# One block for the first projections, and attention joined with its output projection

## The chip, the cores and the metric

The kernel runs on one core of one Trainium2 chip. The metric is the device time of one execution in microseconds (us). The engines are named as in the profile: PE is the matrix engine (PEld its weight loads), DVE the vector engine, ACT the scalar engine, POOL the GpSimd engine, SP the engine that here only issues DMAs. Each engine works through its own instruction queue in order; between engines there are semaphores.

## The reference

One encoder layer over 1280 tokens (1024 of a prompt, 256 of a sample), width 1024, in float32:

```python
h = rmsnorm(x, g_mix)
q, k, v, z, xbc, dtf, dtb, ga, gs = split(h @ w_in)
ya = windowed_gqa(q, k, v, sink, bias) @ w_attn_out     # 8 heads, 2 KV heads, window +-128
ys = ssd_branch(z, xbc, dtf, dtb, conv...) @ w_ssd_out  # conv over time, bidirectional scan, gated norm
x = x + (sigmoid(ga) * ya + sigmoid(gs) * ys) @ w_out
x = x + hier_moe(rmsnorm(x, g_ffn))                     # 16 experts, 2 per token
x = x + sigmoid(rmsnorm(x, g_ple) @ w_ple_gate) * (p @ w_ple_proj)
return rmsnorm(x, g_final)
```

The change lies in the first two lines of the mixers: the projections of `h`, the attention, and the product with `w_attn_out`.

## The kernel before

Every float32 product is made of three passes: each operand is split into a high part (a rounded copy) and a low part (the rest), and high x high, high x low and low x high are summed in PSUM. Weights come in units of 128 x 1024 numbers (512 KB). For each unit SP loads the raw numbers, ACT copies the high part (`split`), and POOL subtracts to get the low part (`rest`, a TENSOR_TENSOR). A ring of two slots (`raw`, `whi`, `wlo`, built by `weight_ring`) carries the units; a slot is loaded again when POOL has read it.

The stages run in this order, each inside a block of its own. At the end of a block every engine waits until all have finished, and a stage usually has its SP queue wait for its last stores before that.

1. `stage_norm_project_z`: normalises and transposes `h`, then multiplies it with eight resident units of `z` in 24 tiles (three groups of token tiles times eight channel tiles), `silu` on ACT after each, and stores them. After tile 19 PE makes the 32 `dt` channels, and after the last tile it transposes them; DVE copies the result to `dt_raw` (L1169).
2. `stage_project_conv`: ten channel tiles of `xbc` (`product`, 8 k-tiles x 3 passes x 3 column groups of 512, 512 and 256 tokens), a convolution on DVE, `silu` on ACT, transposes on PE. Then two "early" tiles of the next stage's columns. It starts with a warm-up of PE (L176) while the first units are loaded and split.
3. `stage_project_rest`: twenty more tiles of the same kind (`q`, `k`, `v` and the gates), two PSUM buffers. Woven into PE's order are small products for the scan's decays: `product(0)`, `decays.tensor`, `product(1)`, `decays.tensor_rows`, and so on. `decays.tensor` waits for a chain of about sixteen small DVE and ACT steps (`Decays.vector`, L555 to L574), which itself waits for two small parameter loads, `dec_bias` and `dec_alog` (L540, L541). POOL's order is `rest(2)`, `rest(3)`, `pool_line`, `rest(4)`, ... where `pool_line` (L766, L770) waits for a line of the bias table that PE makes after `product(3)`.
4. `stage_attention`: PE warms up, makes the scores of unit 0 (a unit is a token tile and half of the heads; there are 20), transposes V in ten steps with two PSUM banks, and makes the scores of unit 1. DVE makes the statistics of unit 0 (`stats`), then copies the ten V tiles (L1404), then makes the statistics of unit 1. ACT takes the exponentials of a unit when its statistics are ready. In the loop, PE transposes the probabilities, ACT copies them out, PE weighs V with them, DVE scales. The attention result of a token tile is turned by PE (`out`), its high part taken by ACT and its low part by DVE. POOL splits the first two units of `w_attn_out` here (`next_hi`, `next_lo`); SP loads them at token tile 1.
5. All semaphores are cleared between two barriers (`clear_semaphores`, L134).
6. One block for `stage_out_att`, the scan and what follows. `stage_out_att` has eight channel tiles of 4 k-tiles x 3 passes over all 1280 tokens; SP loads a gate row, ACT takes its sigmoid (after loading the Sigmoid table, L1458), DVE multiplies (L1494, L1496). PE's tile c waits for DVE's tile c-2.

Several stage functions can add code to one block: then each engine runs the first function's instructions and goes on to the second's with no barrier between.

## Time and profile before

| | us |
|---|---|
| median of 3 runs | 1876.85 (1872.38 to 1877.21) |
| the profiled execution | 1874.15 |
| its span | 1872.3 |
| PE busy in the span | 1743.8 (93%) |
| DVE, ACT, POOL busy | 893.0, 596.7, 410.5 |

Times in the rows below are counted from the start of the span; 1.85 us of the profiled execution lie outside it. The columns PEclk in a table of stretches and in the page give the TensorE clock that was granted: 1.00 is 2.4 GHz and 0.50 is 1.2 GHz. A bracket at the end of a row says how long the engine sat idle before it and what ended the wait.

### The profile page before, as it was taken

To read this page: it belongs to the slowest core of one execution; us is meant where nothing else is said; L and a number is where in the kernel's file an instruction comes from. 1 tells how busy PE (TensorE), PEld (TensorE's weight loads), DVE (VectorE), ACT (ScalarE), POOL (GpSimd) and SP (SyncE) were. 2 spreads that over 40 slices of the span, in tenths; PEclk is the share of its full clock that TensorE was granted. 3 is DMA by queue.
4 is the path that set the end of the run, shared out by engine and by line. 5 is a ranking of instruction groups with operands and counts; after the bars stand their busy time and mean duration, and the time that the engine had idled before them with its cause. 6 is when DMAs were issued, how large, how long until landed. Compare 5 with 4: busy or idle time off the path is not lost. (4 is left out here: it accounts for less than half of the span.)

```text
span 1872.3 us, 27121 instructions
## 1 busy us (share of the span) xinstructions
PE 1743.8 (93%) x10458; PEld 1430.1 (76%) x10459; DVE 893.0 (48%) x1037; ACT 596.7 (32%) x1001; POOL 410.5 (22%) x278
## 2 busy tenths in 40 slices
PE   6998999898999979989999999998899998998897
PEld 5876888786877757768788888787677876786686
DVE  5200777301133216751488522512767787940675
ACT  4201222231111115652355412312534443443332
POOL 3001111112111110001010013000155555652330
PEclk8999999999999989989899999999899998998899
DMA  5212222223345421006666344323857776752552
GB/s 195 88 34 69 68 84 76 106 62 123 117 156 175 130 91 40 28 10 191 201 190 192 115 139 147 101 74 90 314 192 269 255 284 235 296 191 97 173 191 90
DMA packets 115836, 265.90 MB, mean 142 GB/s; under 512 B 13011, under 2 KB 59555, under 8 KB 115740
## 3 DMA queue, kind: packets, MB, share of 16 engines
q1 hardware_dynamic: 99484, 209.11, 34.1%
q0 software_dynamic: 8320, 30.43, 4.8%
q10 hardware_dynamic: 7936, 25.01, 3.7%
q8 instruction: 70, 1.15, 0.3%
q14 instruction: 26, 0.21, 0.0%
HBM read 192.95 MB, written 71.55 MB: 141 GB/s over the span
## 5 line engine op out<-in xcount | busy, mean ns | idle before, releaser
L2078 DVE TENSOR_TENSOR ex_wlo<-ex_raw,ex_whi 128x1024 fp32r<-128x1024 f32 x102 | 168.6, 1667 | 6.0 <-ACT ex_whi L2072 6.0
L286 PE MATMUL rest_p<-hi_h,whi_in 128*128 128x512 f32 (+1 forms) x480 | 123.3, 366 | 12.1 <-POOL wlo_in L905 6.7
L2655 PE MATMUL rt_p<-ex_whi,ex_xh 128*128 x280 | 115.6, 413 | 13.8 <-issue 7.5
L2074 DVE CAST ex_whi<-ex_raw 128x1024 fp32r<-128x1024 f32 x96 | 95.4, 999 | 65.2 <-DMA ex_raw<-experts 60.6
L286 PE MATMUL rest_p<-lo_h,whi_in 128*128 128x512 f32 (+1 forms) x480 | 120.9, 361 | 0.0
L286 PE MATMUL rest_p<-hi_h,wlo_in 128*128 128x512 f32 (+1 forms) x480 | 120.7, 360 | 0.0
L2657 PE MATMUL rt_p<-ex_whi,ex_xl 128*128 x280 | 111.7, 399 | 0.0
L2656 PE MATMUL rt_p<-ex_wlo,ex_xh 128*128 x280 | 111.6, 398 | 0.0
L286 PEld LDWEIGHTS rest_p<-hi_h,whi_in 128*128 128x128 f32 x480 | 81.1, 191 | 34.4 <-POOL wlo_in L905 7.6
L876 ACT ACTIVATE rest_out<-rest_p 128x1024 f32<-128x1024 f32 x20 | 20.5, 1025 | 256.6 <-PE rest_p L286 256.6
L905 POOL TENSOR_TENSOR wlo_in<-wraw_in,whi_in 128x1024 fp32r<-128x1024 f32 x18 | 43.7, 2431 | 222.0 <-ACT whi_in L870 222.0
L286 PEld LDWEIGHTS rest_p<-lo_h,whi_in 128*128 128x128 f32 x480 | 80.7, 190 | 14.4
L286 PEld LDWEIGHTS rest_p<-hi_h,wlo_in 128*128 128x128 f32 x480 | 80.5, 190 | 14.3
L2611 POOL TENSOR_TENSOR ex_xl<-ex_xs,ex_xh 128x1024 fp32r<-128x1024 f32 x35 | 85.9, 2455 | 14.5 <-ACT ex_xs L2057 13.9
L468 DVE SCALAR_TENSOR_TENSOR conv_acc<-xpad,conv_w,conv_acc 128x1284 f32<-128x1284 f32 x40 | 81.7, 2042 | 5.0 <-DVE conv_acc L464 0.3
L1285 PEld LDWEIGHTS pv_p<-v_tok,probs_t 128*128 128x128 f32 x480 | 62.1, 198 | 25.1 <-ACT probs_t L1338 15.2
L1285 PE MATMUL pv_p<-v_tok,probs_t 128*128 128x65 f32 x480 | 68.4, 281 | 10.8 <-ACT probs_t L1338 7.9
L2655 PEld LDWEIGHTS rt_p<-ex_whi,ex_xh 128*128 128x128 f32 x280 | 53.9, 193 | 31.9 <-issue 21.3
L286 PE MATMUL xbc_p<-hi_h,whi_in 128*128 128x512 f32 (+1 forms) x288 | 72.7, 361 | 2.2 <-POOL wlo_in L412 2.2
L1117 PE MATMUL z_p<-hi_h,z_hi 128*128 128x512 f32 (+1 forms) x192 | 70.6, 368 | 4.4 <-DVE lo_h L1151 4.4
L286 PE MATMUL xbc_p<-lo_h,whi_in 128*128 128x512 f32 (+1 forms) x288 | 71.9, 358 | 0.0
L286 PE MATMUL xbc_p<-hi_h,wlo_in 128*128 128x512 f32 (+1 forms) x288 | 71.8, 358 | 0.0
(387 smaller groups left out, 4049.7 us busy)
## 6 DMA issues: line engine op xcount, KB each, us to landing
ex_raw<-experts SPq DMA_DIRECT2D x96, 512.0 KB, 6.2
wraw_in<-units SPq DMA_DIRECT2D x36, 512.0 KB, 4.0
y_slots<-ex_y ACTq DMA_DIRECT2D x35, 512.0 KB, 3.7
rest<-rest_out SPq DMA_DIRECT2D x20, 640.0 KB, 5.7
scan_e<-erow SPq DMA_DIRECT2D x32, 256.0 KB, 4.5
xtok<-conv_tok SPq DMA_DIRECT2D x10, 640.0 KB, 3.3
z_x<-x SPq DMA_DIRECT2D x10, 512.0 KB, 4.1
ao_gate<-rest SPq DMA_DIRECT2D x8, 640.0 KB, 5.2
```

Source lines behind the costliest of these rows:

```text
L286: mm = pe.matmul(out[:, n, 0:size], w[:, kk, :], h[:, kk, c:c + size], start=(kk == 0 and w is whi and h is hi), stop=(kk == ktiles - 1 an ...
L468: mm = dve.scalar_tensor_tensor(out=cv[:, s, :], in0=xpad[:, s, w:w + CONV_LEN], scalar=cw[:, ds(c, 1), w:w + 1], in1=cv[:, s, :], op0=ALU ...
L876: act.activation(got[:, s, 0:1024].rearrange("p (a n) -> p a n", a=2), gp[s][:, 0:2, :], ACT.Copy)
L905: pool.tensor_tensor(wlo[:, s, :], raw[:, s, :], whi[:, s, :].bitcast(F32), ALU.subtract).then_inc(w_lo, 1)
L1117: pe.matmul(out, w.hi[u][:, col], hi[:, kk, tok], start=(kk == 0), stop=False)
L1285: mm = pe.matmul(pv[:, i, :], pt[:, j % 4, b * P:(b + 1) * P], vn[:, n + n // QB + b, i // 2, :], start=(b == 0), stop=(b == 2))
L2074: eng.tensor_copy(self.hi[:, e % 2, n, :], self.raw[e % 2][:, n, :]).then_inc(self.w_hi[n], 1)
L2078: eng.tensor_tensor(self.lo[:, e % 2, n, :], self.raw[e % 2][:, n, :], self.hi[:, e % 2, n, :].bitcast(F32), ALU.subtract).then_inc(self.w ...
L2611: pool.tensor_tensor(xl[s][:, :, :], xs[s][:, :, :], xh[s][:, :, :].bitcast(F32), ALU.subtract).then_inc(x_lo, 1)
L2655: pe.matmul(gu[s][:, :], xh[s][:, kk, :], hi, start=(kk == 0), stop=False)
L2656: pe.matmul(gu[s][:, :], xh[s][:, kk, :], lo, start=False, stop=False)
L2657: mm = pe.matmul(gu[s][:, :], xl[s][:, kk, :], hi, start=False, stop=(kk == KT - 1))
```

## The change

The stages `z`, `conv` and `rest` become one block. The semaphores are cleared after it, and attention moves into the block of `stage_out_att`. Between the stages there are now semaphores where the barriers were:

- the first two `xbc` units are loaded and split within the `z` stage after tile 19, and their low parts made on POOL; the warm-up before `xbc` is gone;
- the first product of `rest` waits for what the `conv` stage left in its PSUM buffers and ring; its two loads follow on SP's queue, each after POOL has read the slot (`first_lo`);
- POOL's `rest(4)` stands ahead of `pool_line`;
- V is copied by ACT; SP loads the first `w_attn_out` units at token tile 3;
- tiles 0 and 1 of `stage_out_att` are made by column groups: columns 0 to 1023 before the last token tile of attention is turned (`last_out`), columns 1024 to 1279 after.

```diff
 stage_project_conv
+        def load_first(sp):
+            for n in range(2):
+                sp.dma_start(raw[:, n, :], d["units"][U_XBC + n]).then_inc(w_in[n], 16)
+        def split_first(act):
+            for n in range(2):
+                act.wait_ge(w_in[n], 16)
+                act.activation(whi[:, n, :], raw[:, n, :], ACT.Copy).then_inc(w_hi, 1)
+        z_tile, z_silued, z_stored, dt_kept = project_z(load_first, split_first)
...
-            sp.wait_ge(stored[0], 96)
-            sp.wait_ge(stored[1], 96)
-            sp.wait_ge(early_stored, 16 * EARLY)
...
-            act.preload_act_table(ACT.Silu)
...
+            rest(0, 0)
+            rest(1, 1)
+            pool.wait_ge(z_tile, 24)
             pool.memset(xpad[:, :, :], 0.0).then_inc(pads, 1)
...
-            warm_up(pe, k, gp[0][:, 0, :], 4)
             product(0, 0, first=True)
+            pe.wait_ge(z_silued, 24)
+            pe.wait_ge(dt_kept, 1)
 stage_project_rest
-            load(2, 0)
-            load(3, 1)
+            for s in range(2):
+                sp.wait_ge(first_lo, 2 + 12 + s + 1)
+                load(2 + s, s)
             decays.sync(sp)
...
             decays.scalar_first(act)
+            act.wait_ge(early_stored, 16 * EARLY)
             copy(0, 0, 1)
...
             rest(2, 0)
             rest(3, 1)
+            rest(4, 0)
             tables.pool_line(pool)
-            with pool.Fori(2, n_tiles // 2) as i:
+            rest(5, 1)
+            with pool.Fori(3, n_tiles // 2) as i:
...
-                pe.wait_ge(w_lo, c + 3)
-                pe.wait_ge(copied, c + 1)
+                if c < 2:
+                    pe.wait_ge(first_lo, 2 + 12 + c + 1)
+                    pe.wait_ge(early_copied, c + 1)
+                else:
+                    pe.wait_ge(w_lo, c + 3)
+                    pe.wait_ge(copied, c + 1)
...
             product(0, 0)
+            pe.wait_ge(tok_copied, 33)
             decays.tensor(pe)
 stage_norm_project_z
+                if n == 19:                        # SP
+                    sp.wait_ge(tile_done, 20)
+                    load_next(sp)
...
+                if n == 20:                        # ACT
+                    act.wait_ge(tile_done, 20)
+                    split_next(act)
                 silu(n)
 stage_attention
-            sp.wait_ge(v_zero, 2)
+            sp.wait_ge(v_zero, 1)
...
-                if n == 1:
+                if n == 3:
                     for u in range(2):
                         sp.dma_start(next_raw[:, u, :], d["units"][U_AO + u]).then_inc(next_in, 16)
...
-            out(NT - 1)
+        def last_out(pe):
+            n = NT - 1
+            pe.wait_ge(att_done, 2 * n + 2)
+            pe.wait_ge(att_lo_s, n)
+            for m in range(4):
+                mm = pe.transpose(ap_[:, m, :], att[:, n % 2, m * P:(m + 1) * P], ident)
+            mm.then_inc(att_turned, 1)
...
+            act.wait_ge(ones_set, 1)               # ACT, ahead of its unit loop
+            for t in range(NT):
+                act.wait_ge(v_turned, t + 1)
+                at = t + 1 if t < QB else t + 2
+                act.activation(vn[:, at, :, 0:HEAD], tp[t % 2][:, 0:P].rearrange(...), ACT.Copy).then_inc(v_copied, 1)
...
             stats(0)
-            for t in range(NT):                    # DVE
-                ...
-                dve.tensor_copy(vn[:, at, :, 0:HEAD], tp[t % 2][:, 0:P].rearrange(...)).then_inc(v_copied, 1)
             stats(1)
 stage_out_att
+        sp.wait_ge(att_turned, 4 * 2 * NT)
         load_gate(0)
...
+        def part(c, n):
+            size = 512 if n < 2 else 256
+            ...
+            for kk in range(4):
+                for a, b in ((w, hi), (w, lo), (wl, hi)):
+                    mm = pe.matmul(gp[c][:, n, 0:size], a[:, kk, :], b[:, kk, 512 * n:512 * n + size], ...)
+        pe.wait_ge(first_split, 4)
+        pe.wait_ge(att_lo_s, 8)
+        for c in range(2):
+            for n in range(2):
+                part(c, n)
+        last_out(pe)
+        pe.wait_ge(att_lo_s, NT)
+        for c in range(2):
+            part(c, 2).then_inc(mm_done, 1)
+        for c in range(2, KT):
-        for c in range(KT):
 build
-    stage_norm_project_z(k, hi, lo)
-    stage_project_conv(k, hi, lo, ring)
-    stage_project_rest(k, hi, lo, q, ring)
+    with k.nc.Block() as block:
+        ...                                        # z, conv and rest, all in this block
-    stage_attention(k, att_hi, att_lo, ring)
     k.clear_semaphores()
...
+                    done = stage_attention(k, inner, block, att_hi, att_lo, ring)   # inside the block after
```

## Rows read from the trace of the kernel before

**Rows 1.** Timeline (start, duration, engine, operation, idle before): from `z` to `conv`.
```profile
124.53 0.60 ACT L1054 ACTIVATE z_out<-z_p 128x512 f32<-128x512 f32 x1 [4.84 <-PE z_p L1119]
160.93 0.49 DVE L1169 COPY dt_raw<-dt_p 128x320 f32<-128x320 f32 x1 [61.37 <-PE dt_p L1135]
171.36 0.85 PE L286 MATMUL xbc_p<-hi_h,whi_in 128*128 128x512 f32 x3 [2.21 <-POOL wlo_in L412]
```

**Rows 2.** Timeline: from `conv` to the first products of `rest`.
```profile
353.91 2.34 POOL L412 TENSOR_TENSOR wlo_in<-wraw_in,whi_in 128x1024 fp32r<-128x1024 f32 x1 [12.78 <-ACT whi_in L366]
356.90 1.41 PE L286 MATMUL rest_p<-hi_h,whi_in 128*128 128x512 f32 x3 [5.34 <-ACTq L863]
358.12 0.43 SPq L541 DMA_DIRECT2D dec_alog<-a_log  x1
362.41 0.49 DVE L555 TENSOR_TENSOR dec_w<-dt_raw,dec_bias 128x320 f32<-128x320 f32 x1 [5.72 <-DMA dec_alog<-a_log]
371.72 0.33 DVE L574 TENSOR_SCALAR ssd_dta<-ssd_minus_dta 128x320 f32<-128x320 f32 x1
373.16 1.25 PE L627 MATMUL rest_spare<-ssd_dta,const 128*128 128x160 f32 x6
374.00 0.98 PE L286 MATMUL rest_p<-hi_h,whi_in 128*128 128x512 f32 x3
...
388.39 0.28 PE L645 MATMUL rest_spare<-const,ssd_dta 128*16 128x128 f32 x1
```

**Rows 3.** Busy time by engine, granted clock, DMA share, GB/s in one stretch.
```profile
356.00:360.00 4.00, 3.10 (x8) 2.58 (x9) 0.07 (x1) 1.28 (x1) 0.24 (x1) 0.50 0.51 146
```

**Rows 4.** Timeline: the stall of tile 4 of `rest`.
```profile
407.56 1.06 ACT L870 ACTIVATE whi_in<-wraw_in 128x1024 fp32r<-128x1024 f32 x1
...
429.28 1.44 PE L286 MATMUL rest_p<-hi_h,whi_in 128*128 128x512 f32 x3 [6.72 <-POOL wlo_in L905]
```

**Rows 5.** Line views of both barriers of the clearing (count, duration, first and last start).
```profile
L136 SPq DRAIN  x3: 7/7/7, 841.5 to 1724.0; - x3
L138 SPq EVENT_SEMAPHORE  x3: 17/17/17, 843.0 to 1725.1; - x3
```

**Rows 6.** Waits of PE, whole span: us, times, longest.
```profile
PE att_tp L1305 <- DVE v_tok L1404: 6.5, 4, 6.0
```

**Rows 7.** Timeline: attention's first units.
```profile
693.36 0.44 PE L1305 MATMUL att_tp<-const,v_ch 128*128 128x128 f32 x2
699.54 2.13 ACT L1330 ACTIVATE scores<-scores,att_stat 128x384 f32<-128x384 f32 x4 [13.53 <-DVE att_stat L1377]
702.97 2.93 PE L1264 MATMUL score_p<-k_win,q_blk 64*128 64x384 f32 x8
705.95 1.76 DVE L1367 SCALAR_TENSOR_TENSOR scores<-score_p,bias 128x1536 f32<-128x1536 f32 x1 [2.58 <-PE score_p L1264]
```

**Rows 8.** Line views (count: shortest, median, longest ns) in attention.
```profile
L1338 ACT ACTIVATE probs_t<-att_tp x80: 465/490/493, 706.6 to 833.0; 128x384 f32<-128x384 f32 x80
L1377 DVE TENSOR_TENSOR att_stat<-att_stat,sink x20: 161/161/2189, 697.3 to 826.2; 128x4 f32<-128x4 f32 x20
```

**Rows 9.** Timeline: POOL's subtraction beside that line.
```profile
697.12 2.37 POOL L1251 TENSOR_TENSOR wlo_in<-wraw_in,whi_in 128x1024 fp32r<-128x1024 f32 x1
```

**Rows 10.** Timeline: end of attention and the first output tiles.
```profile
835.18 1.06 PE L1295 MATMUL att_t<-const,att_tok 128*128 128x128 f32 x4
839.54 0.60 ACT L1342 ACTIVATE hi_att<-att_t 128x512 fp32r<-128x512 f32 x1 [2.67 <-PE att_t L1295]
...
843.06 1.28 ACT L1458 ACT_TABLE_LOAD   x1 [2.92 <-PEq L138]
849.77 1.27 ACT L1461 ACTIVATE ao_gate<-ao_gate 128x1280 f32<-128x1280 f32 x1 [0.27 <-DMA ao_gate<-rest]
858.99 1.23 DVE L1494 TENSOR_TENSOR ao_prod<-ao_p,ao_gate 128x1024 f32<-128x1024 f32 x1 [5.48 <-PE ao_p L286]
860.13 0.41 DVE L1496 TENSOR_TENSOR ao_prod<-ao_p,ao_gate 128x256 f32<-128x256 f32 x1
```

More of the change, by code:

```diff
@@ L288, in pe_channel_tile, with stage_project_conv @@
     return mm
-def stage_project_conv(k, hi, lo, ring):
+def stage_project_conv(k, ctx, block, hi, lo, ring, project_z):
     nc, d = k.nc, k.d
-    with ExitStack() as ctx:
+    if True:
         raw, whi, wlo = ring
@@ L458, in _ @@
             dve.wait_ge(cw_in, 16)
+            for s in range(4):
+                dve.wait_ge(z_stored[s], 96)
             def conv(c, s):
@@ L487, in _ @@
             tokens(9, 1, 4)
+    return stored, ch_stored, early_copied, early_stored, w_lo, tok_copied
 class SsdTiles:
@@ L802, in vector, with stage_project_rest @@
         dve.memset(bias[:, 2, :, 2 * P:], NEG)
-def stage_project_rest(k, hi, lo, q, ring):
+def stage_project_rest(k, ctx, block, hi, lo, q, ring, xt_stored, ch_stored, early_copied, early_stored, first_lo, tok_copied):
     nc, d = k.nc, k.d
     n_tiles = 22 - EARLY
-    with ExitStack() as ctx:
+    if True:
         raw, whi, wlo = ring
         got = k.at("rest_out", [P, 2, T], F32, O_ST)
+        gp = [ctx.enter_context(nc.psum_tensor(f"rest_p{s}", [P, 3, 512], F32)) for s in range(2)]
         spare = [ctx.enter_context(nc.psum_tensor(f"rest_spare{n}", [P, 512], F32)) for n in range(2)]
@@ L917, in _ @@
             decays.vector(dve)
+            dve.wait_ge(ch_stored, 16)
+            for s in range(2):
+                dve.wait_ge(xt_stored[s], 96)
             tables.vector(dve, states.free)
@@ L969, in pe_token_tile, with stage_norm_project_z @@
     return mm
-def stage_norm_project_z(k, hi, lo):
+def stage_norm_project_z(k, ctx, block, hi, lo, load_next, split_next):
     nc, d = k.nc, k.d
@@ L1168, in _, with stage_attention @@
             dve.wait_ge(dt_turned, 1)
-            dve.tensor_copy(k.dt_raw[:, :, :], dp[:, :, :])
-def stage_attention(k, att_hi, att_lo, ring):
+            dve.tensor_copy(k.dt_raw[:, :, :], dp[:, :, :]).then_inc(dt_kept, 1)
+    return tile_done, silued, stored, dt_kept
+def stage_attention(k, ctx, block, att_hi, att_lo, ring):
     nc, d = k.nc, k.d
     UNITS = 2 * NT
-    with ExitStack() as ctx:
+    if True:
         o = O_R1 + 10 * 4096
@@ L1415, in _, with stage_out_att @@
             rest(NT - 1)
-def stage_out_att(k, ctx, block, hi, lo, ring, early):
+    return last_out, att_lo_s, turned, next_split
+def stage_out_att(k, ctx, block, hi, lo, ring, early, last_out, att_lo_s, att_turned, first_split):
     nc, d = k.nc, k.d
@@ L1474, in _ @@
     def _(pe):
-        for c in range(KT):
+        def part(c, n):
+            size = 512 if n < 2 else 256
+            w, wl = (x[:, 0, c * 4 * P:(c + 1) * 4 * P].rearrange("p (k c) -> p k c", k=4) for x in (whi, wlo))
+            for kk in range(4):
+                for a, b in ((w, hi), (w, lo), (wl, hi)):
+                    mm = pe.matmul(gp[c][:, n, 0:size], a[:, kk, :], b[:, kk, 512 * n:512 * n + size],
+                                   start=(kk == 0 and a is w and b is hi), stop=(kk == 3 and a is wl))
+            return mm
+        pe.wait_ge(first_split, 4)
[8 more added lines that the diff above has]
+        for c in range(2, KT):
             u = c // 2
@@ L2991, in out_att @@
                 with ExitStack() as inner:
-                    return stage_out_att(k, inner, block, att_hi, att_lo, ring, early)
+                    done = stage_attention(k, inner, block, att_hi, att_lo, ring)
+                with ExitStack() as inner:
+                    return stage_out_att(k, inner, block, att_hi, att_lo, ring, early, *done)
             done = stage_ssd_scan(k, ctx, block, y_hi, y_lo, so_ring, out_att)
```

52 lines of the change are left out of this document (26 added, 26 removed).

## The prediction

> **What bounds the kernel now.** I read the page first: PE is busy in 93% of the span, every other engine in under half, so the kernel is paid for in PE's order of work, and what can be won cheaply is what PE idles. The waits of PE over the whole span come next; there the reader is to see that the long waits of the first half lie on few places, such as the transposes of V, which waited 6.5 us for DVE's copies [rows 6]. The timelines around those places then show who was late. Between the places PE is dense: in `conv`, in `rest` and in the output tiles a product follows a product, and work that is moved off other engines there is worth nothing. The table of stretches adds a second price: after 5.34 us of idling the first products ran at a granted clock of 0.50 [rows 2, 3], so a pause costs its own length and then a slow start. A product of `rest` at full clock takes 388.39 - 374.00 = 14.39 us, the one behind the pause 373.16 - 356.90 = 16.26: the slow start costs 1.87 [rows 2].
>
> **The change part by part.** All times are on the clock of the old trace; a gain is how much earlier PE reaches the same instruction.
>
> *From z to conv.* PE started the first `xbc` product at 171.36, after a block end, a load, a split and a subtraction on POOL [rows 1]. Now the two loads leave after tile 19, whose `silu` ran at 124.53; loading, splitting and subtracting have over 30 us beside dense PE work and cost nothing. SP's queue gets two loads, ACT two copies ahead of a `silu` that waits for PE anyhow. What is late next: the product waits for `padded`, which DVE raises only behind its copy to `dt_raw`, 160.93 + 0.49 = 161.42. With a handover of 0.2 PE starts at 161.6: gain 9.7 (10.4 with no handover and no copy in the way, 9.2 with a handover of 0.7). The clearing of `xpad` on POOL waits for the last tile, but its reader comes a product later.
>
> *From conv to rest.* The first product of `rest` started at 356.90, 5.34 after `conv` ended at 351.56 [rows 2]. Its unit was split and its buffer copied long before, so now it starts at 351.6 with a warm clock and ends at 351.6 + 14.39 = 366.0, 7.2 before the old 373.16. But `decays.tensor` is next in PE's queue and needs DVE's chain, and the chain needs `dec_alog`. On SP that load stands behind `load(3)`, which now waits for POOL's subtraction to end at 353.91 + 2.34 = 356.25; two more issues of 0.43 put it at 357.2, only 0.9 before the old 358.12. With the old flight of 362.41 - 358.12 = 4.29 it lands at 361.5; one 512 KB load fewer is right ahead, so I take 360.5. The chain lasts 371.72 + 0.33 - 362.41 = 9.64, so PE goes on at 370.2, after a pause of 4.2. `decays.tensor` took 374.00 - 373.16 = 0.84; at half clock I put 1.3, so product 1 starts at 371.5 instead of 374.00. Of these 2.5 the slow start takes 1.9 back: gain 0.5 (-0.5 with the old flight, 3.3 if the load is quick and the clock holds). So here one pause is traded for another. The added wait for `tok_copied` is long satisfied; the wait for the early stores stands in ACT's queue ahead of `copy(0)`, behind the chain's last exponential step, with the stores landed by then.
>
> *The order on POOL.* Tile 4 of `rest` waited 6.72 us because POOL sat in `pool_line`, though the high part was there at 407.56 + 1.06 = 408.6 [rows 4]. With `rest(4)` ahead, its low part is ready some 11 us before PE wants it: gain 6.72 and the slow start, 8.6 (8.0 to 8.8). `pool_line` is not delayed, since it waits for tile 3's end; `rest(5)` follows it with a whole product to spare.
>
> *The clearing.* It moves from behind attention to behind `rest`. From the first barrier to the end of the second took 843.0 - 841.5 = 1.5 us here and 1.1 at the last place [rows 5]. The old end of `rest` had a plain block end, so attention starts 1.5 later: -1.5 (-1.1 to -1.6). The clearing behind attention is counted below.
>
> *V on ACT.* ACT idled 13.53 us before the first exponentials [rows 7], so the copies are beside nothing that ends last. PE transposes V from 693.36. A copy of 128 x 128 is not in the trace; a copy three times as wide takes 0.49 [rows 8], so ten take at most 4.9 and at least a third of it, and I put 4.5 with the handovers. Then the scores of unit 1 run from 698.0, for 2.93 at half clock as before or half of that at full, and `stats(1)` starts at 699.5 to 701 instead of 705.95; the first exponentials need only `stats(0)`, and follow at 698. Gain 4.9 to 6.4; I take 5.7, and 4.5 as the lowest. `stats(1)` leads the later units, so it carries through.
>
> *The weight split inside the loop.* POOL's copies and subtractions for `w_attn_out` now fall into the unit loop. In the trace DVE's small addition L1377 took 2189 ns once against a median of 161, from 697.32 on, while POOL's subtraction ran from 697.12 to 699.49 [rows 8, 9]. ACT's exponentials waited for it [rows 7], so this is on the path. Two subtractions of 2.37 fall into a loop in which such small operations come once in (826.2 - 697.3) / 19 = 6.8 us: a chance of about 0.7, with half of 2.37 each time, is 0.8; I take -1.0 (0 to -2.4, as both can hardly be hit fully). The Trainium skill (SBUF, State Buffer, section Who interferes with whom) says that a vector operation with two SBUF inputs and a GpSimd operation that reads SBUF lock each other out whole, and one with a single SBUF input does not; by it only L1374 and L1377 are exposed and the term stays at 1.0, while without it the 1.76 us of L1367 [rows 7] could be hit too and the term would be near its end of -2.4. The row of L1377 agrees; no row here shows a safe operation beside that subtraction in the unit loop.
>
> *Attention into its projection.* The old PE finished `out(8)` at 835.18 + 1.06 = 836.24 and reached output tile 2 at 858.99, DVE's start on tile 1 [rows 10]. Now four parts of 12 passes of 512 columns follow at once: 14.39 us for 24 x 1280 columns gives 0.240 per 512 or 11.5, and 1.9 for a slow start: 849.6. Then `last_out` (0.6 at full clock) and ACT's high part (0.60) until 850.8. ACT's queue has the Sigmoid table (1.28) and the first sigmoid (1.27) only behind that: 853.4. DVE's product (1.23 + 0.41) ends at 855.0, and PE, done with its two short parts by 854.4, waits for it. Gain 4.0 (3.0 if ACT's handovers add up, 5.9 if neither the table nor the slow start shows).
>
> The sum is 9.7 + 0.5 + 8.6 - 1.5 + 5.7 - 1.0 + 4.0 = 26.0 us. From the profiled execution, 1874.15, that leaves 1848.1. This execution lies 2.7 under the median of the runs shown, from which it would be 1850.9; I predict 1849.
>
> **The rivals.**
> - *The decays are not late.* The parameter loads land early enough or the clock survives the pause: 2.8 more, 1846. For it: they are 16 KB each. Against: the queue order, which holds them to 357.2.
> - *The clock stays low through the token parts.* Attention's last transposes and weighings ran at half clock, and if the parts don't raise it, their 11.5 take 23: 9.6 more, 1859. Against: behind the pause of rows 3 dense products had it back within a product.
> - *The first stage change does nothing.* If the two units are still not split when `z` ends, 9.7 are lost: 1859. For it: the loads wait in SP's queue behind stores. Against: they have 30 us.
> - *The unbroken run is throttled.* `z`, `conv` and the start of `rest` now run without a pause: from tile 19 at 124.53 to 366 that is over 240 us, where `conv` alone ran 351.56 - 171.36 = 180 [rows 1, 2]. If the granted clock fell to half beyond 180, the last 60 would take 120: 60 - 26 = 34 slower, 1908. It decides from a mean grant under 60 / (60 + 26) = 0.70 in those 60. For it: no row shows such a run. Against: each fall behind which I saw a slow start came after idling, as in rows 2 and 3.
>
> **How the numbers follow.** Chances: the forecast 0.68; decays in time 0.12; clock low in the parts 0.08; first change void 0.05; throttled run or a like loss 0.03; half of the gains lost in some way not named 0.04, which leaves about 1862. The low ends of the terms add to 9.2 - 0.5 + 8.0 - 1.6 + 4.5 - 2.4 + 3.0 = 20.2, the high ends to 10.4 + 3.3 + 8.8 - 1.1 + 6.4 - 0 + 5.9 = 33.7; they will not all fall on one side. From 1874.15 and from the median that spans 1840 to 1857. I give 1840 to 1859, which takes in the two rivals at 1859 and leaves out the slow one and the last. What a measurement of this kernel can tell from no change is about 0.3%, 5.6 us: faster by more 0.95, within 0.02, slower 0.03.
>
> **What would show it.** Right: no warm-up and under 1 us of PE idling between the `dt` transposes and `xbc`; PE waiting some 4 us for DVE at `decays.tensor` with the grant at 0.50 behind it; no wait of tile 4 for POOL; V's transposes running through within 5 us; DVE's L1374 or L1377 once near 1 to 2 us; PE dense from `out(8)` to output tile 2 but for about 2 us. Wrong: a pause elsewhere of the same size as one removed, above all inside `rest` or at the start of the scan, or a granted clock under 1.00 in a dense stretch.

## The result, and the profile after

The changed kernel took 1843.26 us (median of 4 runs, 1834.84 to 1844.89) against 1874.62 us for the kernel before (4 runs, 1866.73 to 1877.21) on the same chip: a ratio of 0.9844, 95% interval 0.9809 to 0.9879, or some 31 us less. The forecast was 1849, 26.0 less than before. The profiled execution spans 1840.8 us where the old one spanned 1872.3.

To see where the time came from, I took the same instruction in both traces and noted how much earlier it starts now (the lead). The gain of a part is the growth of the lead across it.

| PE or ACT reaches | before | after | lead | gain of the part | predicted |
|---|---|---|---|---|---|
| first `xbc` product | 171.36 | 160.91 | 10.45 | 10.3 (`z` itself ended 0.2 earlier) | 9.7 |
| first `rest` product | 356.90 - 5.34 idle | 340.93 | 10.6 | 0.2, `conv` | 0 |
| end of tile 3 of `rest` | 421.53 | 410.44 | 11.1 | 0.5 | 0.5 |
| end of `rest`, last copy | 679.09 | 659.41 | 19.7 | 8.6 | 8.6 |
| attention's warm-up | 683.85 | 665.54 | 18.3 | -1.4 | -1.5 |
| `stats(1)` | 705.95 | 680.02 | 25.9 | 7.6 | 5.7 |
| last exponential of the unit loop | 827.95 | 803.55 | 24.4 | -1.5, of it -0.9 by the held operation | -1.0 |
| output tile 2 | 858.71 | 824.97 | 33.7 | 9.3 | 4.0 |
| end of the span | 1872.3 | 1840.8 | 31.5 | -2.2 | 0 |

Most groups of rows of the old kernel have an answer in the new trace. *From z to conv* [rows 1], timeline (start, duration, engine, line, operation, idle before and its releaser):

```profile
160.73 0.49 DVE L1200 COPY dt_raw<-dt_p 128x320 f32<-128x320 f32 x1 [61.36 <-PE dt_p L1166]
160.91 0.83 PE L286 MATMUL xbc_p<-hi_h,whi_in 128*128 128x512 f32 x3 [0.22 <-DVEq L463]
```

No warm-up and no wait for POOL is left: PE idles 0.22 us, for the increment that stands in DVE's queue behind the `dt_raw` copy.

*From conv to rest* [rows 2], the same view:

```profile
340.93 0.75 PE L286 MATMUL rest_p<-hi_h,whi_in 128*128 128x512 f32 x3
...
346.74 0.42 SPq L554 DMA_DIRECT2D dec_alog<-a_log  x1
350.42 0.49 DVE L568 TENSOR_TENSOR dec_w<-dt_raw,dec_bias 128x320 f32<-128x320 f32 x1 [22.53 <-DMA dec_alog<-a_log]
359.73 0.33 DVE L587 TENSOR_SCALAR ssd_dta<-ssd_minus_dta 128x320 f32<-128x320 f32 x1
360.20 2.47 PE L640 MATMUL rest_spare<-ssd_dta,const 128*128 128x160 f32 x6 [5.04 <-DVE ssd_dta L587]
362.00 1.74 PE L286 MATMUL rest_p<-hi_h,whi_in 128*128 128x512 f32 x3
```

And by stretches (us, busy time of PE, PE's loads, DVE, ACT, POOL, then the granted clock, DMA share, GB/s), as in [rows 3]:

```profile
340.00:355.00 15.00, 15.00 (x78) 12.62 (x76) 3.76 (x8) 4.70 (x7) 2.41 (x1) 1.00 0.39 120
...
360.00:364.00 4.00, 3.80 (x11) 3.15 (x12) 0.55 (x2) 2.56 (x5) 2.12 (x1) 0.51 0.00 0
364.00:375.00 11.00, 11.00 (x58) 9.36 (x57) 2.00 (x18) 0.00 (x0) 0.23 (x1) 1.00 0.38 109
```

The first product of `rest` runs at once at a grant of 1.00. Then PE waits 5.04 us for DVE's chain, and the grant behind the wait is 0.51, as behind the old pause. The old pause went and came back a product later.

*Tile 4 of rest* [rows 4] follows the line's product (410.44 to 411.4) without a wait:

```profile
411.39 0.85 PE L286 MATMUL rest_p<-hi_h,whi_in 128*128 128x512 f32 x3
```

*Attention's first units* [rows 7] (V's copies, the scores of unit 1, its statistics), and the place in the loop where POOL's work met DVE's [rows 9]:

```profile
675.55 0.45 ACT L1388 ACTIVATE v_tok<-att_tp 128x128 f32<-128x128 f32 x2 [7.85 <-PE att_tp L1338]
...
678.41 1.56 PE L1297 MATMUL score_p<-k_win,q_blk 64*128 64x384 f32 x8
...
679.29 2.13 ACT L1370 ACTIVATE scores<-scores,att_stat 128x384 f32<-128x384 f32 x4 [0.50 <-DVE att_stat L1423]
...
680.02 1.76 DVE L1413 SCALAR_TENSOR_TENSOR scores<-score_p,bias 128x1536 f32<-128x1536 f32 x1 [0.76 <-PE score_p L1297]
...
701.57 2.36 POOL L1283 TENSOR_TENSOR wlo_in<-wraw_in,whi_in 128x1024 fp32r<-128x1024 f32 x1
...
703.86 1.04 POOL L1281 CAST whi_in<-wraw_in 128x1024 fp32r<-128x1024 f32 x1
703.88 1.05 DVE L1420 SCALAR_TENSOR_TENSOR att_stat<-att_stat,nsink 128x4 f32<-128x4 f32 x1
```

Two of V's tiles take ACT 0.70 from start to start (675.55 to 676.25 and so on), so all ten are done in 3.2. The scores of unit 1 run in 1.56, at full clock, where the old ones took 2.93. In the loop the small operation L1420 takes 1.05 instead of 0.16, and it ends when POOL's cast does (704.90). That is a hold as forecast, but by the cast: the prediction had counted only the subtractions.

*The end of attention* [rows 10]. First the stretches from the last exponential: of the kernel after, of the kernel before, and of a second profile of the kernel before (`before_again` below):

```profile
803.60:808.50 4.90, 3.97 (x37) 3.73 (x35) 0.00 (x0) 2.37 (x7) 0.00 (x0) 1.00 0.17 32
808.50:819.50 11.00, 11.00 (x51) 9.05 (x50) 1.36 (x4) 0.60 (x1) 0.00 (x0) 1.00 0.27 107
819.50:825.00 5.50, 3.77 (x30) 3.31 (x28) 2.33 (x4) 4.32 (x4) 0.00 (x0) 1.00 0.00 0
```

```profile
827.90:839.10 11.20, 8.12 (x41) 7.49 (x38) 1.43 (x5) 3.06 (x8) 0.00 (x0) 0.56 0.00 0
```

```profile
826.60:834.30 7.70, 4.61 (x39) 4.08 (x38) 1.40 (x5) 3.04 (x8) 0.00 (x0) 1.00 0.00 0
```

The low grant of 0.56 at the old end of attention is absent from the second profile of the same kernel (1.00). So the change need not have won that part: from the last exponential to the end of `out(8)` the two old profiles take 8.3 and 5.2 us, and the new one 5.2. From the end of `out(8)` to output tile 2 they take 22.5 and 22.6, and the new one 16.2. The new handover itself, in the timeline (`last_out`'s transposes run from 819.51 to 820.1):

```profile
820.14 0.60 ACT L1382 ACTIVATE hi_att<-att_t 128x512 fp32r<-128x512 f32 x1 [10.77 <-PE att_t L1357]
820.76 1.28 ACT L1501 ACT_TABLE_LOAD   x1
...
821.52 0.38 PE L1523 MATMUL ao_p<-hi_att,whi_in 128*128 128x256 f32 x1 [1.41 <-DVE lo_att L1442]
...
823.36 1.22 DVE L1555 TENSOR_TENSOR ao_prod<-ao_p,ao_gate 128x1024 f32<-128x1024 f32 x1 [1.90 <-ACT ao_gate L1504]
...
824.97 0.85 PE L286 MATMUL ao_p<-hi_att,whi_in 128*128 128x512 f32 x3 [0.32 <-DVE ao_prod L1557]
```

*What was given back.* From the first gather of the experts to the last product of its stage the lead fell from 36.4 to 31.7. (From output tile 2 to that gather it had grown by 2.7; the second pair of profiles below does not show that growth.) The waits of PE (total, times, longest) name the place: POOL's product `ex_hid`, 8.9 us at the longest where the old kernel has 5.3. First after, then before:

```profile
PE pp_p L2741 <- POOL ex_hid L2676: 10.8, 2, 8.9
```

```profile
PE pp_p L2680 <- POOL ex_hid L2615: 7.2, 2, 5.3
```

One such product takes 11.31 us on POOL where the other 34 of this trace take 0.73 to 1.72, beside a run of casts and subtractions on DVE, which the timeline shows without a hole up to 1532.2:

```profile
1521.51 11.31 POOL L2676 TENSOR_TENSOR ex_hid<-ex_up,ex_silu 128x256 f32<-128x256 f32 x1 [7.14 <-ACT ex_up L2771]
...
1529.89 2.34 DVE L2139 TENSOR_TENSOR ex_wlo<-ex_raw,ex_whi 128x1024 fp32r<-128x1024 f32 x2
...
1542.25 0.69 DVE L2135 CAST ex_whi<-ex_raw 128x1024 fp32r<-128x1024 f32 x1 [10.01 <-DMA ex_raw<-experts]
```

In the old trace the same product took 7.17 us:

```profile
1557.17 7.17 POOL L2615 TENSOR_TENSOR ex_hid<-ex_up,ex_silu 128x256 f32<-128x256 f32 x1 [7.26 <-ACT ex_up L2710]
```

It ended inside DVE's run, beside a cast that came a little late: that cast (1563.79) began 0.03 us behind the end of the subtraction before it, while the others of that run start some 0.1 before the subtraction ends. In the second old profile the late cast still starts 0.04 before that end, and the product took 7.17 there too; so a late start goes with the way in, and a full hole is not shown to be needed.

### The profile page after: what moved, and what is told of

Read it like the earlier page. It is cut to its first block and busy times, and to the rows that moved or that the text cites. A ratio compares the mean times of both kernels' runs of the same rounds, so it can differ in the third digit from the quotient of the medians.

```text
span 1840.8 us, 27069 instructions
## 1 busy us (share of the span) xinstructions
PE 1726.6 (94%) x10450; PEld 1417.9 (77%) x10451; DVE 885.6 (48%) x1027; ACT 597.5 (32%) x1010; POOL 414.3 (23%) x278
## 3 DMA queue, kind: packets, MB, share of 16 engines
q8 instruction: 70, 1.15, 0.3%
## 5 line engine op out<-in xcount | busy, mean ns | idle before, releaser
L920 POOL TENSOR_TENSOR wlo_in<-wraw_in,whi_in 128x1024 fp32r<-128x1024 f32 x18 | 43.8, 2434 | 230.5 <-ACT whi_in L883 230.5
L2672 POOL TENSOR_TENSOR ex_xl<-ex_xs,ex_xh 128x1024 fp32r<-128x1024 f32 x35 | 85.9, 2456 | 16.2 <-ACT ex_xs L2118 15.7
L412 POOL TENSOR_TENSOR wlo_in<-wraw_in,whi_in 128x1024 fp32r<-128x1024 f32 x14 | 36.1, 2585 | 204.2 <-ACT whi_in L370 152.2
L1318 PEld LDWEIGHTS pv_p<-v_tok,probs_t 128*128 128x128 f32 x480 | 59.7, 191 | 26.6 <-ACT probs_t L1378 16.6
```

What stands on the lines that cost most here:

```text
L920: pool.tensor_tensor(wlo[:, s, :], raw[:, s, :], whi[:, s, :].bitcast(F32), ALU.subtract).then_inc(w_lo, 1)
L1318: mm = pe.matmul(pv[:, i, :], pt[:, j % 4, b * P:(b + 1) * P], vn[:, n + n // QB + b, i // 2, :], start=(b == 0), stop=(b == 2))
L2672: pool.tensor_tensor(xl[s][:, :, :], xs[s][:, :, :], xh[s][:, :, :].bitcast(F32), ALU.subtract).then_inc(x_lo, 1)
```

## The experiments

The ratios are against runs of the kernel before on the same chip in the same hours (medians 1876.88, 1876.06 and 1872.85 for the three groups). Where two kernels were in different groups I compare ratios, not times.

**Both kernels again.**

> The changed kernel once more, unaltered. Theory A: PE's granted clock in the last two units of attention is an accident of each execution, not a product of the change; then this trace may show it at 1.00 or 0.50 there, and out(8) moves by some 2.7 us with it. Theory B: the change keeps the clock up there; then it is 1.00 again. Either way the waits of the first trace return: PE 5.0 us at decays.tensor, no wait of tile 4 of rest, L1420 or L1423 hit once. Time as before, about 31 us under the kernel before.

> The kernel before once more, unaltered, for a second trace. Theory A: the granted clock in the last two units of attention may be 1.00 or 0.50; theory B: 0.50 again. If the experts' stage (first ex_x to last) differs from the first trace's 355.2 us by several us, then the 4.7 us that the changed kernel seems to lose there is noise; if it stays near 355, the loss is a result of the change.

After: 1843.97 (5 runs, 1841.76 to 1847.07), ratio 0.9824 (0.9809 to 0.9839). Before: 1870.32, one run with a profile. Against this second pair of profiles the total lead is 1858.0 - 1831.4 = 26.6 us at the last product of the kernel, near the forecast's 26.0. The differences to the first pair lie where they should by the reading above: the first unit's exponentials start 5.8 behind its scores and not 7.7 (no held L1377 this time; the longest is 165 ns), and the end of attention ran at a grant of 1.00. These two, 1.9 and 3.1, are nearly all of the 4.9 between the pairs. But this old execution is 6.6 under the median of its group, so the pair shows less than the medians, which are 32.9 apart. The loss in the experts comes back: from the first gather to the last product of the stage the old kernel takes 372.4 and 372.9, the changed one 377.1 and 375.7, and its product is held for 11.31 us both times. So it is no noise of one profile.

**The decay parameters early.** The two 16 KB loads are issued in `conv`, ahead of its last early store:

```
             for n in range(EARLY):
+                if n == EARLY - 1:
+                    params(sp)
                 sp.wait_ge(early_copied, n + 1)
...
-            decays.sync(sp)
```

> The changed kernel with the two parameter loads (dec_bias, dec_alog) issued on SP ahead of the second early store, so no longer behind load(3). Theory: the 5.0 us wait at decays.tensor is owed to the place of these loads alone; the chain then starts when ACT has loaded its table at about 344.7 and ends at about 353, before product 0 ends at 355.2, so the wait goes, the clock stays at 1.00 there, and the time falls by 5 to 6.5 us against the changed kernel. Rival: the chain of DVE and ACT steps itself is too long, and a wait of 2 us or more stays.

1835.36 us (5 runs, 1831.31 to 1839.32), ratio 0.9776 (0.9757 to 0.9794); in the same group as the changed kernel, 8.6 less than its median. In the timeline the tables' product now starts behind the first product of `rest` with no idling, and the next at nearly full clock:

```profile
353.94 0.74 PE L286 MATMUL rest_p<-hi_h,wlo_in 128*128 128x512 f32 x3
354.52 1.25 PE L642 MATMUL rest_spare<-ssd_dta,const 128*128 128x160 f32 x6
...
355.36 0.98 PE L286 MATMUL rest_p<-hi_h,whi_in 128*128 128x512 f32 x3
```

From the first product of `rest` to its end the trace has 311.4 us instead of 318.5: 7.1 less, the 5.04 and the slow clock behind it. So the queue order on SP was what held the decays. Not all of the 8.6 is theirs, though: in this program POOL's held product of the experts took 7.17 again, and its block 17.5 instead of 21.4 and 21.8, while the scores of unit 1 were slow (2.93 us).

**Whole output tiles.** Tiles 0 and 1 are begun whole behind `last_out`, not by token ranges:

```
         pe.wait_ge(first_split, 4)
-        pe.wait_ge(att_lo_s, 8)
-        for c in range(2):
-            for n in range(2):
-                part(c, n)
         last_out(pe)
         pe.wait_ge(att_lo_s, NT)
-        for c in range(2):
-            part(c, 2).then_inc(mm_done, 1)
-        for c in range(2, KT):
+        for c in range(KT):
```

> The changed kernel with tiles 0 and 1 of stage_out_att made whole again, after last_out; everything else as changed, attention still in the same block. Theory A (clock and barrier made the large gain at attention's end, the column groups only about 2 us): slower by 2 to 2.5 us than the changed kernel. Theory B (the column groups made most of the 7 us between out(8) and output tile 2): slower by 5 us or more.

1850.04 us (4 runs, 1848.04 to 1856.62), ratio 0.9867 (0.9847 to 0.9887): 6.1 over the median of the changed kernel in the same group, and the intervals are apart. Without the parts PE has a hole of 1.39 us of work in 5.0, and the grant falls and is low into the output tiles:

```profile
808.10:813.10 5.00, 1.39 (x8) 0.78 (x6) 2.06 (x5) 1.97 (x3) 0.00 (x0) 0.65 0.59 239
813.10:829.00 15.90, 15.90 (x73) 13.42 (x74) 1.56 (x2) 3.10 (x4) 0.00 (x0) 0.90 0.26 80
```

From the last exponential to the last output product it takes 68.1 us, against 64.0 in the changed kernel and 70.3 and 73.3 in the two profiles of the kernel before. So by the traces, of the 6.3 against the second old profile 4.1 are the parts', and 2.2 come from the shared block. By the time the parts are worth 6.1, which is theory B; the trace lies between the two theories.

**The order on POOL alone.** The kernel before, with `rest(4)` and `rest(5)` placed around `pool_line` as in the change:

```
             rest(3, 1)
+            rest(4, 0)
             tables.pool_line(pool)
-            with pool.Fori(2, n_tiles // 2) as i:
+            rest(5, 1)
+            with pool.Fori(3, n_tiles // 2) as i:
```

> The kernel before, with one part of the change alone: POOL subtracts for tiles 4 and 5 of the rest before and right behind pool_line. Theory A (PE waited only for that low part, and nothing is late next): tile 4 starts without a wait, the end of the rest comes 8.6 us earlier, as between the traces of before and after (lead 11.1 to 19.7), and the whole kernel 8.6 us earlier, 1868 against 1877. Rival B (pool_line itself becomes late and something in the decay tables waits for it): the gain at the end of the rest is under 4, and PE shows a new wait between tile 5 and attention. Rival C (the granted clock moves instead): tile 4 starts at once but some stretch behind it runs at 0.50, and the gain is 6.7 or less.

1860.57 us (7 runs, 1850.58 to 1870.96), ratio 0.9912 (0.9880 to 0.9944). The trace has what theory A says: from the first product of `rest` to its end 313.4 instead of 322.2, 8.8 less, and of PE's two waits in the stage, 6.7 and 5.3, only the latter is left:

```profile
PE rest_p L286 <- ACTq L863: 5.3, 1, 5.3
```

The time fell by more than that (0.88% is 16 us; the lower end of the interval is 0.56%, 10.5 us). I have no trace that shows the rest of it: the profiled run, the slowest of the seven, is only 3.4 us under the old span. It reached `rest` 3.4 late, and lost 4.7 in the experts, where the product was held for 10.37 us. What makes the medians differ by 16 stays open.

**V back on DVE.** The changed kernel with V's copies moved from ACT to DVE, behind `stats(0)`:

```
-            act.wait_ge(ones_set, 1)
-            for t in range(NT):
-                act.wait_ge(v_turned, t + 1)
...
             stats(0)
+            dve.wait_ge(ones_set, 1)
+            for t in range(NT):
+                dve.wait_ge(v_turned, t + 1)
+                at = t + 1 if t < QB else t + 2
+                dve.tensor_copy(vn[:, at, :, 0:HEAD], tp[t % 2][:, 0:P].rearrange("p (g e) -> p g e", g=N_KV)
+                                ).then_inc(v_copied, 1)
             stats(1)
```

> The changed kernel with one part undone: V is copied by DVE behind stats(0), as before, not by ACT. Theory A (the copies stood between stats(0) and stats(1) on DVE, and that is all): the second unit's bias addition starts 5 to 6 us later than in the changed kernel, the lead at the end of the unit loop falls by as much, and the time is 1849 to 1850 against 1844. Rival B (all of the 7.6 us that the trace showed between warm-up and the second unit is the copies'): 1851.6. Rival C (DVE's copies cost nothing beside ACT's, and the gain was that POOL's subtraction no longer fell on the first unit's small addition, 1.9): 1846. Where POOL's subtractions fall now is open to a shift by up to 2.4 either way.

1846.23 us (6 runs, 1831.02 to 1856.04), ratio 0.9849 (0.9804 to 0.9893); too wide to tell any of these numbers from the changed kernel's. The trace tells: PE waits for DVE in V's transposes again, and `stats(1)` starts at 685.20, with the first scores 0.2 earlier than in the changed kernel at 680.02, so 5.4 later:

```profile
678.97 0.49 DVE L1444 COPY v_tok<-att_tp 128x128 f32<-128x128 f32 x2
...
679.32 0.69 PE L1338 MATMUL att_tp<-const,v_ch 128*128 128x128 f32 x2 [3.96 <-DVE v_tok L1444]
...
685.20 1.76 DVE L1407 SCALAR_TENSOR_TENSOR scores<-score_p,bias 128x1536 f32<-128x1536 f32 x1 [2.28 <-PE score_p L1297]
```

At the last exponential (807.8 against 803.6, again counted from the first scores) 4.5 of it are left. That is theory A by the trace, not by the time. Here the held product of the experts took 7.19 and not 11.31, which hides most of it at the end of the span.

**The split at another place.** The projection's two loads are issued at pair 1 and not at pair 3 (`if n == 3:` becomes `if n == 1:` in SP's loop).

> The changed kernel with the projection's two loads issued at pair 1 and not at pair 3, so that POOL's two subtractions of 2.36 us fall elsewhere in the unit loop. Theory A (a small DVE operation with two inputs from SBUF is held by a subtraction of POOL, and only such a one): the one long DVE operation of the loop (1.05 us on L1420) is gone from its place, and there is one again only if a subtraction overlaps L1420 or L1423; the time stays within 2 us of 1844. Rival B (the 0.9 us lost in the loop came from the loads' traffic or from ACT's two copies, not from POOL): the loss moves to the new place with the same 0.9 and no long DVE operation there.

1845.80 us (6 runs, 1841.69 to 1849.32), ratio 0.9843 (0.9813 to 0.9874). The hold moved with POOL, onto the first unit:

```profile
678.09 1.04 POOL L1281 CAST whi_in<-wraw_in 128x1024 fp32r<-128x1024 f32 x1 [9.07 <-DMA wraw_in<-units]
678.22 1.75 DVE L1418 TENSOR_REDUCE att_stat<-scores 128x4 f32<-128x1536 f32 x1
679.21 2.35 POOL L1283 TENSOR_TENSOR wlo_in<-wraw_in,whi_in 128x1024 fp32r<-128x1024 f32 x1
680.00 1.57 DVE L1420 SCALAR_TENSOR_TENSOR att_stat<-att_stat,nsink 128x4 f32<-128x4 f32 x1
681.50 1.03 POOL L1281 CAST whi_in<-wraw_in 128x1024 fp32r<-128x1024 f32 x1
681.61 0.94 DVE L1423 TENSOR_TENSOR att_stat<-att_stat,sink 128x4 f32<-128x4 f32 x1
682.47 1.75 DVE L1413 SCALAR_TENSOR_TENSOR scores<-score_p,bias 128x1536 f32<-128x1536 f32 x1
682.61 2.36 POOL L1283 TENSOR_TENSOR wlo_in<-wraw_in,whi_in 128x1024 fp32r<-128x1024 f32 x1
```

Read it in pairs. The reduction (one input, 1.75) runs beside POOL's cast and subtraction at its usual length; so does L1413, which reads PSUM and SBUF, beside the second subtraction. Only L1420 and L1423, with both inputs in SBUF, are held, the first until the subtraction ends, the second until the cast does. ACT's exponentials start 2.2 later relative to the scores than in the changed kernel (7.8 against 5.7), PE waits 2.27 for them, and behind that the grant is 0.75 from 682 to 690 and 0.86 from 690 to 700: at the last exponential the loop is 4.6 behind the changed kernel's, counted from the first scores. The medians don't show it. Theory A, except that a cast on POOL holds the small operations too, as it did in the changed kernel.

**Both, with last_out between the parts.** Early parameters, and `last_out(pe)` behind the first two parts instead of behind all four:

```
-        for c in range(2):
-            for n in range(2):
-                part(c, n)
-        last_out(pe)
+        part(0, 0)
+        part(0, 1)
+        last_out(pe)
+        part(1, 0)
+        part(1, 1)
```

> The changed kernel with the decay parameters loaded early (1835 when run alone) and last_out moved between the first two token parts and the second two. Theory A (ACT's high part, table and sigmoids then lie beside the second two parts, and only DVE's first product of 1.2 + 0.4 us stands between the parts and output tile 2): tile 2 starts 1.7 us earlier relative to the end of the unit loop, no PE wait on lo_att, 1833.7. Rival B (last_out's place doesn't matter, since output tile 2 waits for DVE in any case): 1835. Rival C (the earlier arrival lengthens the unbroken run of DVE's casts in the experts, and POOL's product of 0.7 us there is held for 11.3 us again and not 7.2): 1838.

1835.78 us (6 runs, 1831.57 to 1839.16), ratio 0.9786 (0.9756 to 0.9817): not to be told from the early parameters alone. In the trace it takes 15.06 us from the end of `out(8)` to output tile 2 instead of 16.21, and PE has no wait on `lo_att`: 1.15 of the 1.7, with a low clock just before (0.63), so nearer to theory A than to rival B. Rival C did not come: the held product took 7.23. But this execution lost more earlier than it could win there. L1424 was held 2.30 us by POOL's subtraction at 698.04, PE paused, and the grant fell to 0.50 behind it (columns as above):

```profile
690.00:704.00 14.00, 11.20 (x83) 8.58 (x81) 11.92 (x15) 8.04 (x19) 6.74 (x4) 0.95 0.26 96
704.00:712.00 8.00, 8.00 (x34) 6.21 (x34) 1.46 (x4) 3.09 (x7) 0.00 (x0) 0.50 0.01 2
```

The unit loop, first to last exponential, took 130.0 us here against 124.7 with the early parameters alone. A hold of 2.3 us thus cost about 5. For the question asked there is this one trace, and no time.

**The split on DVE.** On top of the early parameters, the loop's two casts and two subtractions go from POOL to DVE, one behind the statistics of each of units 10 to 13:

```
                 stats(u)
+                if 10 <= u < 14:
+                    n = (u - 10) // 2
+                    dve.wait_ge(next_in, 32)
+                    if u % 2 == 0:
+                        dve.tensor_copy(next_hi[:, n, :], next_raw[:, n, :]).then_inc(next_split, 1)
+                    else:
+                        dve.wait_ge(next_split, 2 * n + 1)
...
```

> The changed kernel with the decay parameters loaded early (1835 when run alone), and the split of the projection's first two units inside the unit loop is done by DVE, one operation of 0.7 or 1.2 us behind the statistics of units 10 to 13, and not by POOL. Theory A (POOL's subtraction held a small DVE operation with two inputs from SBUF, 0.9 us and in other runs 2.2 and 2.3, and the pause could bring a low clock behind it): no operation on L1420 or L1423's counterparts over 0.3 us, the loop from the first to the last exponential takes 124 us or less at a granted clock of 1.00, and the time is 0 to 3 us under 1835. Rival B (DVE has no room there): the operations delay the scaling behind them by their length, the loop is 2 to 4 us longer, 1838.

1828.12 us (6 runs, 1821.85 to 1836.12), ratio 0.9763 (0.9725 to 0.9802). In the lines (count: shortest, median, longest ns) no small operation is held any more, and the loop takes 123.4 us at a grant of 1.00:

```profile
L1415 DVE SCALAR_TENSOR_TENSOR att_stat<-att_stat,nsink x20: 161/163/164, 671.5 to 793.4; 128x4 f32<-128x4 f32 x20
L1418 DVE TENSOR_TENSOR att_stat<-att_stat,sink x20: 161/161/165, 671.7 to 793.6; 128x4 f32<-128x4 f32 x20
```

The gain over the early parameters alone (0.9776) is not resolved by the time. The loop is 1.3 shorter by the trace, but that is not the split's: in the trace of the early parameters the scores of unit 1 ran slow, here they take 1.56:

```profile
671.18 2.93 PE L1298 MATMUL score_p<-k_win,q_blk 64*128 64x384 f32 x8
```

Against the two profiles of the changed kernel, which also have 1.56 there, the loop is 0.9 and 0.7 shorter, about what their held operation had cost (0.9 and 0.6). That is theory A.

**Holes in the experts' run on DVE.** The changed kernel, with each subtraction right behind its own cast, so that it waits for the cast to end:

```
-                ew.split_hi(dve, e, 0)
                 for n in range(6):
+                    ew.split_hi(dve, e, n)
...
-                    if n < 5:
-                        ew.split_hi(dve, e, n + 1)
                     ew.split_lo(dve, e, n)
```

> The changed kernel, and in the experts DVE subtracts each weight unit right behind its own cast, not behind the next unit's cast, so that every subtraction waits for a cast to be finished and DVE has a short hole in each pair. Theory A (in the changed kernel a product of 0.7 us on POOL is held for 11.31 us, to the end of an unbroken run of DVE's casts and subtractions, and PE waits 8.9 us for it): with a hole in each pair POOL gets in at the next hole, the longest ex_hid on POOL is under 3 us, the block interval of 21.4 us falls to about 12 to 14 and the kernel is 5 to 9 us faster than the changed one, 1836 against 1844. The holes cost DVE 0.1 to 0.2 us in each of 102 pairs, beside waits for the weights' transfers. Rival B (POOL waits for something else that ends at the same time, such as the weights' transfers): the longest product stays at 7 to 11 us and the time within 3 us of 1844. Rival C (DVE's holes make the weights late): the long product is gone, but PE waits for ex_wlo instead, 1850.

1833.16 us (6 runs, 1824.30 to 1836.82), ratio 0.9785 (0.9750 to 0.9819), against 0.9824 (0.9809 to 0.9839) and 0.9844 (0.9809 to 0.9879) for the changed kernel; the intervals overlap, so it is the trace that decides. In the timeline POOL's product, issued in the middle of the same run, gets in:

```profile
1527.30 0.69 DVE L2135 CAST ex_whi<-ex_raw 128x1024 fp32r<-128x1024 f32 x1
1527.32 1.26 POOL L2674 TENSOR_TENSOR ex_hid<-ex_up,ex_silu 128x256 f32<-128x256 f32 x1 [6.62 <-ACT ex_up L2769]
...
1528.02 1.64 DVE L2139 TENSOR_TENSOR ex_wlo<-ex_raw,ex_whi 128x1024 fp32r<-128x1024 f32 x1
```

No `ex_hid` takes over 2 us; the block of 21.4 us takes 9.8, better than the 12 to 14 expected; PE's longest wait for it is 1.6. A pair takes DVE 1.86 us from start to start (1522.43 to 1524.30 and on) where it took 1.74: the holes cost 0.12 each. Theory A; PE's longest wait for `ex_wlo` is 2.7, against 2.8 in the changed kernel, so the weights don't come late.

**The three together** (early parameters, split on DVE, holes):

> The last two together with the early parameters: the changed kernel with the decay parameters loaded early, the split in the unit loop on DVE, and the holes between DVE's casts and subtractions in the experts. Theory A (the three are independent, and the experts lose 4 to 7 us to the held product here too): 1828, 7 us under the early parameters alone. Rival B (the held product is hidden by the weights' transfers once PE comes earlier): 1834.

1826.22 us (6 runs, 1819.40 to 1827.71), ratio 0.9746 (0.9714 to 0.9779). This is the fastest kernel here, 2.5% under the old one; against `split_dve` the 1.9 us of the medians are not resolved. In its profiled run attention's end drew the low clock again (0.57 between 797.5 and 805.5), and the last output product came 6.8 us later than in `split_dve`; yet the last product of the kernel came 4.1 earlier, so the stages behind gained 10.9, above all the block of 20.0 us that takes 10.2. Theory A.

## Why the prediction was right

The time fell inside the range, and most of the steps came as forecast. The total was 5 us too cautious by the medians; two terms were off, one at the projection and one at zero that should not have been, and some agreement is luck, as said below.

- *From z to conv* (9.7): 10.3. What I named as late next, DVE's queue behind the `dt_raw` copy, is what ends PE's wait, but the increment was issued at 160.75 while the copy ran until 161.22. The price with the copy's end in the way was 0.5 too low.
- *From conv to rest* (0.5): 0.5, by two errors that cancel. The pause of 4.2 was 5.04: the load was issued at 346.74, as the queue order said (10.6 of lead: 357.3 on the old clock), and landed 3.7 later, but the chain took 350.42 to 360.06 and PE's handover 0.14 more, while product 0 ended a little earlier. The small products of `decays.tensor` took 1.80 and not 1.3, so product 1 started 1.1 later than forecast; but it took 15.30, only 0.9 and not 1.9 over its 14.39. `params_early` shows that the pause was worth 7.1, so the rival with the decays in time was real, and priced far too low at 2.8; only the queue kept it away.
- *POOL's order* (8.6): 8.6 in the pair of traces, 8.8 alone.
- *The clearing* (-1.5): -1.4.
- *V on ACT* (5.7) *and the split in the loop* (-1.0): together 4.7 predicted; by the lead at the last exponential 6.0 against the first old profile and 22.2 - 17.2 = 5.0 against the second, which had only an operation of 0.33 in it. V alone is 5.4 by `v_dve`. The held operation cost 0.9 in the new trace, near the forecast by luck: the forecast came from the two subtractions and left out the two casts, and it was a cast that held it, here and in most of the other profiles; a subtraction did in `both` and `load_at_1`. By the rule of the Trainium skill that the prediction weighed (SBUF, State Buffer, section Who interferes with whom) only the two small operations are exposed, and to any POOL operation that reads SBUF. `load_at_1` agrees, with the rows of the safe ones beside them, for casts and subtractions. The end of -2.4 was not low enough: with the clock behind it, a hold cost 5 in `both`, and the two in `load_at_1` 4.6.
- *Attention into its projection* (4.0): this is the term that was mis-sized. It runs from the end of `out(8)` to output tile 2, and there it measured 6.3 and 6.4 against the two old profiles (22.5 and 22.6 become 16.2 and 16.2). I charged a slow start of 1.9 for the parts, from an old trace whose attention ended at a grant of 0.56, and the new kernel has none: the grant is 1.00 throughout. Where the clock did fall before the parts (`best`), the stretch took 17.6. The table's 9.3 holds 3.1 more, from the last exponential to `out(8)`, which of the two old profiles only the first shows. `rest4_alone`, with the old attention, is slow there too (8.1 us at a grant of 0.60), so whether the change makes the low clock rarer there is open.
- *What I had at zero*: the experts. I searched the places around the change and did not ask whether a collision 700 us later would shift. It did: a held product of 7.17 us became 11.31, and the block that contains it took 21.4 instead of 17.4. `gap` breaks DVE's run and the hold is gone, so it was the run that held it. The Trainium skill has the ground for it in the same section: a cast on DVE in its two-port mode and a subtraction with two SBUF inputs each take the interface that GpSimd reads through, for the whole instruction. The traces agree in that POOL is held beside these two operations, and add that it got in at none of the boundaries inside the unbroken run; in which mode the casts ran no row shows. That the length follows from the earlier arrival is not shown: in `v_dve` the experts start at about the same time as in the changed kernel (first gather at 1307.6 against 1304.0 and 1308.1), and the product took 7.19.

So in the second pair the total of 26.6 is near the forecast's 26.0 because the projection's extra gain and the experts' loss nearly cancel. The 31 to 33 us of the medians are more than these terms explain for that pair, and which stretch of a typical old execution holds the rest stays open.

Of the rivals, the clock staying low through the parts fell: where the clock was low before them (`both`, 0.63 from 803 to 811), the stretch of the parts ran at 0.97. The unbroken run was not throttled: from 160.91 to 355 PE worked without a pause, and the stretch that ends it ran at a grant of 1.00.

## What to carry to other kernels

When a pause is taken away, look in the next engine queue for what was hidden under it, and for small loads that stand behind a large one there; moving two 16 KB loads ahead was worth as much as most of the planned edits. A second profile of the kernel before tells which of its slow stretches belong to the program and which to one execution; take prices from those that repeat. An unbroken run on one engine can hold a short operation on another to the end of the run, as DVE's casts and subtractions held POOL's product here, and a hole of 0.12 us in each pair was worth more than it cost. And when a forecast term comes out right, look whether its parts did.

## What the hardware showed that I had not expected

- An increment in DVE's queue, with no instruction attached, rose before the copy ahead of it had ended: it was issued at 160.75, PE's next product started at 160.91, and the copy ran from 160.73 to 161.22. So here it was no sign that the copy was done.
- A POOL product that takes 0.73 us at its shortest took 7.2, 10.27, 10.37 or 11.3 us in a run of DVE's casts and subtractions. The longer ones ended 0.6 behind the run's end, the 7.2 beside a late cast inside it. The block around it took 17.0 to 17.5, 20.0, 20.0 and 20.4 to 21.8 us.
- The same stretch of the same program, the end of attention, had a granted clock of 0.56 in one profile and 1.00 in another (kernel before), 0.60 in `rest4_alone`, and 0.57 or 0.63 in two of the ten profiles of kernels with the change, 1.00 in the other eight. The scores of unit 1 took 1.56 us in six of the nine profiles with V on ACT and 2.93 in the other three (`params_early`, `gap`, `best`). What decides either is open.
